# A two-layer hybrid attention backbone on one core: first loads ahead of the semaphore clearing, waits split by operand, and a changed order of work at the ends of phases

## The reference, cut to what matters

```python
for layer in range(DEPTH):
    need_ctx = layer < DEPTH - 1
    h_l = modulate(x, norm1_g[layer], sh1, sc1)        # rmsnorm(x, g) * (1 + scale) + shift
    h_c = modulate(xc, norm1_g[layer], csh1, csc1)
    ...                                                # o_l, o_c: the two attentions of the layer
    x = x + g1 * (o_l @ w_out[layer])
    x = x + g2 * sq_relu_mlp(modulate(x, norm2_g[layer], sh2, sc2), mlp_w1[layer], mlp_w2[layer])
    if need_ctx:
        xc = xc + cg1 * (o_c @ w_out[layer])
        xc = xc + cg2 * sq_relu_mlp(modulate(xc, norm2_g[layer], csh2, csc2), mlp_w1[layer], mlp_w2[layer])
return x

def diff_attend(q, k, v, lam):
    s = jnp.einsum('bqhtd,bkhtd->bthqk', q, k).astype(jnp.float32) * (q.shape[-1] ** -0.5)
    a = jax.nn.softmax(s, axis=-1)
    p = a[:, 0] - lam * a[:, 1]
    return jnp.einsum('bhqk,bkhe->bqhe', p.astype(v.dtype), v)
```

## Time and profile before

| | us |
|---|---|
| three runs before | 3991.56, 3997.02 (median), 3999.05 |
| profiled execution: its own time | 3994.86 |
| its span in the trace | 3993.1 |
| PE busy | 3593.2 (90%) |
| DVE busy | 2000.9 (50%) |
| ACT busy | 1297.3 (32%) |
| POOL busy | 172.7 (4%) |
| mean granted clock of PE | 0.945 |

### The profile page before, as it was taken

One profiled execution on the slowest core, in us unless ns is written; L12 is line 12 of the kernel. 1 busy time (PEld: TensorE's weight loads), 2 busy tenths in 40 slices (PEclk: granted clock), 3 DMA queues, 4 the chain that ended last, 5 costly groups with the idle time before them and its releaser, 6 DMA issues. The chain is left out here.

```text
span 3993.1 us, 47823 instructions
## 1 busy us (share of the span) xinstructions
PE 3593.2 (90%) x17926; PEld 2880.8 (72%) x17926; DVE 2000.9 (50%) x2900; ACT 1297.3 (32%) x2312; POOL 172.7 (4%) x186
## 2 busy tenths in 40 slices
PE   8779798696989999999988889699699889999999
PEld 2567666585778888888867778477466678888887
DVE  2564365586654444443455356488444363333333
ACT  2453244464431111111125445466333351111111
POOL 0200020000120000000001000000000020000000
PEclk9899899898999999999998989799799899999999
DMA  8344453442322222222214344333344331111112
GB/s 306 130 152 161 132 119 86 102 98 78 90 72 68 66 68 59 60 60 60 61 52 154 138 153 136 85 72 71 79 99 90 99 97 48 45 47 47 50 53 69
DMA packets 438709, 370.72 MB, mean 93 GB/s; under 512 B 103302, under 2 KB 382614, under 8 KB 433430
## 3 DMA queue, kind: packets, MB, share of 16 engines
q1 hardware_dynamic: 438549, 368.61, 32.7%
HBM read 280.86 MB, written 87.69 MB: 92 GB/s over the span
## 5 line engine op out<-in xcount | busy, mean ns | idle before, releaser
L2022 DVE SCALAR_TENSOR_TENSOR xT<-ps,mods,xT 128x1024 f32<-128x1024 f32 x192 | 189.3, 1014 | 420.8 <-PE ps L2236 420.8
L2236 PE MATMUL ps<-e_gh,e_w2h 128*128 128x512 f32 x1280 | 355.6, 375 | 5.9 <-DVE e_w2l L2474 3.6
L2236 PE MATMUL ps<-e_gl,e_w2h 128*128 128x512 f32 x1280 | 351.7, 372 | 0.0
L2236 PE MATMUL ps<-e_gh,e_w2l 128*128 128x512 f32 x1280 | 351.3, 372 | 0.0
L2522 DVE TENSOR_TENSOR e_plain<-e_plain 128x1280 f32<-128x1280 f32 (+1 forms) x64 | 86.9, 1358 | 503.7 <-ACT e_plain L2389 503.7
L2236 PE MATMUL ps<-e_hh,e_w1h 128*128 128x512 f32 (+1 forms) x1200 | 329.2, 372 | 7.2 <-DVE e_w1l L2474 7.2
L2236 PE MATMUL ps<-e_hl,e_w1h 128*128 128x512 f32 (+1 forms) x1200 | 328.6, 371 | 0.0
L2236 PE MATMUL ps<-e_hh,e_w1l 128*128 128x512 f32 (+1 forms) x1200 | 328.2, 371 | 0.0
L2389 ACT ACTIVATE e_plain<-ps 128x1280 f32<-128x1280 f32 (+1 forms) x64 | 72.7, 1135 | 777.8 <-PE ps L2236 765.2
L2236 PEld LDWEIGHTS ps<-e_gh,e_w2h 128*128 128x128 f32 x1280 | 224.1, 189 | 55.3 <-DVE e_gl L2526 8.0
L2236 PEld LDWEIGHTS ps<-e_gl,e_w2h 128*128 128x128 f32 x1280 | 225.4, 189 | 43.4
(11 more groups left out here) (347 smaller groups left out, 7493.5 us busy)
## 6 DMA issues: line engine op xcount, KB each, us to landing
e_raw<-in_mlp_w SPq DMA_DIRECT2D x64, 512.0 KB, 4.2
e_raw<-in_mlp_w SPq DMA_DIRECT2D x128, 256.0 KB, 2.9
aw<-in_ada_w SPq DMA_DIRECT2D x12, 2048.0 KB, 9.2
e_raw<-in_w_out SPq DMA_DIRECT2D x48, 512.0 KB, 4.0
rstd<-in_ada_w SPq DMA_DIRECT2D x64, 384.0 KB, 3.4
qkC<-pc_stage SPq DMA_DIRECT2D x72, 192.0 KB, 2.7
hT<-pa_hb SPq DMA_DIRECT2D x10, 1024.0 KB, 5.4
qkA<-pa_stage SPq DMA_DIRECT2D x20, 512.0 KB, 3.2
```

The lines of the kernel that those rows point to most:

```text
L2022: ins = k.nc.vector.scalar_tensor_tensor(out=x, in0=ps, scalar=k.mods[:, layer, gate, bass.ds(n, 1), w], in1=x, op0=ALU.mult, op1=ALU.add)
L2236: mm = pe.matmul(k.ps[:, SB * (e % 2) + b, 0:n], w[:, e % 2, f], m[:, f, c0:c0 + n], start=(f == 0 and x == 0), stop=(f == nf - 1 and x == 2))
```

## The change

1. **Clearing behind loads.** `clear_before` stands behind the first loads in every phase: six weight slices in `pa`, `pb`, `pd`; three tiles of weights, the gains and rope in `pc`; the first head's loads in `ab`, `ac`, `ad`, `aa`; four row tiles and two weight tiles in the two `e`.
2. **Waits by operand.** `load_head` raises a near semaphore (what the rough products read) and a far one (the rest and the values). In `aa`, q's first 512 columns and k of map 0, those of map 1, and the rest (v, q's other columns) have one each, with 13 loads per head in place of 11; in `ac` 5 in place of 3. The score of a head's first step, and the cast of the values, wait for far.
3. **Tables.** `ab`'s two masks are one load, with the sinks behind the first head; `ad`'s three are one; `aa`'s lambda constants come behind the first head.
4. **project's order.** The jobs of tiles 0 and 1 alternate: (0,0), (1,0), (0,1), (1,1), ... The second half of h(2) is built after job 3 (`pa`) or 5 (`pd`) (`split_at`). In `pd` the reciprocals of the norm (L696) are made per 128 tokens, ten in place of three, between the h of the tiles.
5. **layer_end's order.** Row tiles 0, 1 before weight tile 0, tiles 2, 3 before tile 1; roots and norm of a row tile one unit earlier; beside the units only part 0's h is built (u 10 to 13, and 16 to 19 in layer 1), part 1's after the loop; (1,0) before the sums, (0,2)'s weights cut ahead of the first relu; `next_sums` adds the last feature tile's squares by three more matmuls instead of a last accumulation on DVE.

```diff
-    jobs = [(t, j) for t in range(NT) for j in range(U) if t < LT or not units[j].latents]
+    jobs = [(t, j) for j in range(U) for t in range(2)] + [(t, j) for t in range(2, NT) for j in range(U) if t < LT or not units[j].latents]
+    split_at = [first_of[0]] + [max(first_of[t], last_of[t - 1] + 1) for t in range(1, NT)]
...
-                k.phases.clear_before(sp)
...
                     sp.dma_start(raw[:, x % RAW, 0:u.width], w_dram[f, :, col0 + u.c0:col0 + u.c0 + u.width]).then_inc(wr[x % RAW], 16)
+                    if x == RAW - 1:
+                        k.phases.clear_before(sp)
...
-                    if keeps_h and n == first_of[t] and t + 1 < NT:
-                        modulate(t + 1, range(KT // 2, KT))
+                    for x in range(NT - 1):
+                        if keeps_h and n == split_at[x]:
+                            modulate(x + 1, range(KT // 2, KT))
...
+                def inverse(t):
+                    if sums_at is not None and t < NT:
+                        q = slice(t * P, (t + 1) * P)
+                        dve.wait_ge(s.std, t * P // 512 + 1)
+                        nc.vector.reciprocal(k.rstd[:, q], k.rstd[:, q]).then_inc(s.rec, 1)
...
                     if u % NQ == 0:
-                        pe.wait_ge(s.ld0 if p == 0 else s.ld1, i * 16 * loads + 16 * loads)
+                        pe.wait_ge(s.ld0 if p == 0 else s.ld1, i * 16 * near + 16 * near)
...
+                    if x % NS == 0:
+                        pe.wait_ge(s.lf0 if p == 0 else s.lf1, i * 16 * far + 16 * far)
...
-        p, n = u // KT - 1, u % KT
-        return [(p, f) for f in (2 * n - 4, 2 * n - 3)] if p >= 0 and 2 <= n < 2 + KT // 2 else []
+        f = 2 * (u - (KT + 2 if SB == 3 else 2 * KT))
+        return [(0, f), (0, f + 1)] if 0 <= f < KT else []
...
                 fetch_rows(0)
+                fetch_rows(1)
...
                 fetch_out(0)
-                fetch_rows(1)
+                fetch_rows(2)
+                fetch_rows(3)
                 fetch_out(1)
-                for t in range(2, min(nt, RB + 4)):
+                k.phases.clear_before(sp)
+                for t in range(4, min(nt, RB + 4)):
...
-                    t = turned_beside(u)
+                    t = turned_beside(u + 1)
...
-                    pe.wait_ge(s.acc2, KT)
+                    pe.wait_ge(s.x, x_nth(C - 1, KT - 1))
+                    pe.wait_ge(s.acc2, KT - 1)
...
                         early(0, 0)
+                        early(1, 0)
                         sums(NP - 1)
-                        for p in range(1, NP - 1):
+                        for p in range(1, NP):
                             early(0, p)
-                        for p in range(NP - 1):
                             early(1, p)
-                        early(0, NP - 1)
-                        early(1, NP - 1)
```

More of the change, by code:

```diff
@@ L119, in shape_constants @@
     before, after = np.where(c >= q, 0, MASKED), np.where(c <= q, 0, MASKED)
-    out["wmask"] = np.stack([before, after], 1).astype(np.float32)
-    out["wband"] = np.stack([after.T, np.zeros((P, P)), before.T], 1).astype(np.float32)
+    out["wtab"] = np.stack([before, after, after.T, np.zeros((P, P)), before.T], 1).astype(np.float32)
     cq, ck = np.arange(GRID_W)[:, None], np.arange(GRID_W)[None, :]
@@ L125, in shape_constants @@
     col = np.where((ck >= cs) & (ck < cs + NA_COLS), 0, MASKED).astype(np.float32)
-    out["cmask"] = np.concatenate([col, col], 0)
-    out["cmaskT"] = np.tile(col.T, (2, 2))
     first, last = np.zeros((2, P, P), np.float32)
@@ L133, in shape_constants @@
     last[:, GRID_W:] = MASKED
-    out["rmask"] = np.ascontiguousarray(np.stack([first, last, first.T, last.T], 1))
+    out["ntab"] = np.concatenate([first, last, first.T, last.T, np.tile(col.T, (2, 2)), np.concatenate([col, col], 0)], 1).astype(np.float32)
     return out
@@ L720, in _ @@
                         before = None
-                    if keeps_h and n == first_of[t] and t + 1 < NT:
-                        split_h(t + 1)
+                    for x in range(NT - 1):
+                        if keeps_h and n == split_at[x]:
+                            split_h(x + 1)
+                            inverse(x + 2)
                 if before is not None:
@@ L1302, in attend @@
     EB, OB, TB = 5, 6, 7
-    loads = load_head(None, None, None, None, None, None)
+    near, far = load_head(None, None, None, None, None, None)
     last_step = [max(x for x in range(V) if (x // NS) * NB + head_steps[x % NS].block == b) for b in range(BLOCKS)]
@@ L1369, in attend @@
             b_sb, bT = sb("b", [P, 2, BR, GRID_W], F32R), sb("bT", [P, 2, 2, ND, P], F32R)
-            cmask, cmaskT = sb("cm", [P, GRID_W]), sb("cmT", [P, P])
             rmask = sb("rm", [P, 4, P], F32R)
-        mtab = sb("mtab", [P, 5, P]) if sink is not None or bias is not None else None
-        tables = 3 if sink is not None or bias is not None else 0
+        mtab = sb("mtab", [P, 6, P]) if sink is not None or bias is not None else None
+        tables = 2 if sink is not None else 1 if bias is not None else 0
+        if bias is not None:
+            cmaskT, cmask = mtab[:, 4], mtab[:, 5, 0:GRID_W]
         if beside is not None:
@@ L1448, in pair @@
                         fetch(0, 0, False)
+                        if sink is not None:
+                            sp.dma_start(sinks[:], sink.unsqueeze(0).broadcast_to([P, heads])).then_inc(s.tab, 16)
+                        k.phases.clear_before(sp)
                         fetch(0, 1, False)
@@ L1581, in values_high @@
                 def values_high(i, p):
-                    act.wait_ge(s.ld0 if p == 0 else s.ld1, i * 16 * loads + 16 * loads)
+                    act.wait_ge(s.lf0 if p == 0 else s.lf1, i * 16 * far + 16 * far)
                     nc.scalar.copy(vh[:, p], v_sb[:, p]).then_inc(s.vh, 1)
@@ L1743, in stacked_loader, with load @@
 def stacked_loader(qk, q_base, k_index, v_dram, v_index, v_width, n_q):
-    def load(sp, i, p, places, _, sem):
+    def load(sp, i, p, places, near, far):
         if sp is None:
-            return 6
+            return 3, 3
         q_sb, k_sb, v_sb, q_top, k_top = places
@@ L1897, in values @@
                     pe.wait_ge(s.ev, turn_nth(i, v, c))
+                    if c == 0 and v % NQ == 0:
+                        pe.wait_ge(s.lf0 if v < NQ else s.lf1, (i + 1) * 16 * 3)
                     if c == 0 and (i or v):
@@ L2250, in next_sums @@
                 def next_sums():
-                    pe.wait_ge(s.acc2, KT)
+                    pe.wait_ge(s.x, x_nth(C - 1, KT - 1))
+                    pe.wait_ge(s.acc2, KT - 1)
                     for b, (c0, n) in enumerate(chunks):
-                        mm = pe.matmul(k.ps[:, NEXT_BANK + b, 0:n], k.ones[:], sqx[:, 2, c0:c0 + n], start=True, stop=True)
+                        pe.matmul(k.ps[:, NEXT_BANK + b, 0:n], k.ones[:], sqx[:, 2, c0:c0 + n], start=True, stop=False)
+                    pe.wait_ge(s.sq2, KT)
+                    for b, (c0, n) in enumerate(chunks):
+                        mm = pe.matmul(k.ps[:, NEXT_BANK + b, 0:n], k.ones[:], sqx[:, (KT - 1) % 2, c0:c0 + n], start=False, stop=True)
                     mm.then_inc(s.sum2, 1)
@@ L2371, in _ @@
                         modulate(p, f)
+                cut(0, 1, True)
                 square(NU - 1)
+                for f in range(KT):
+                    modulate(NP - 2, f)
                 deviation(NP - 1)
-                cut(0, 1, True)
                 for f in range(KT):
@@ L2380, in chunk @@
                         if e + 1 < U:
-                            if not (first and e == 0):
-                                cut(c, e + 1, first)
+                            if not (first and e == 1):
+                                cut(c, e + 2 if first and e == 0 else e + 1, first)
                         elif not last:
@@ L2503, in _ @@
                 add_out(NU - 1)
+                cut(0, 1)
                 accumulate(NU - 2)
                 accumulate(NU - 1)
+                for f in range(KT):
+                    split(NP - 2, f)
                 inverse(NP - 1)
-                cut(0, 1)
                 for f in range(KT):
@@ L2513, in chunk @@
                         if e + 1 < U:
-                            if not (first and e == 0):
-                                cut(c, e + 1)
+                            if not (first and e == 1):
+                                cut(c, e + 2 if first and e == 0 else e + 1)
                         elif not last:
```

73 lines of the change are left out of this document (36 added, 37 removed).

## The result

| | median us | lowest to highest | ratio to before, 95% interval |
|---|---|---|---|
| before, runs beside this one | 3998.03 | 3991.56 to 3999.14 | |
| changed | 3955.06 | 3952.21 to 3958.08 | 0.9897 [0.9882, 0.9912] |

A forecast was written before the change was run, and what follows sets the result against it. PE bounds the kernel, busy 3593.2 of 3993.1 us; the change can move its idle time and slower running behind pauses. Terms sum to -37.8: 3957 against the profiled 3994.9, 3959 against the median; range 3935 to 3981.

The forecast's parts named there:

- pa: Projection pa: one more job behind the wait for h(1), slower matmuls, later h(2), less the clears: +8.8 us.
- pd: Projection pd: loss between +5 and +10 from the job order, with reciprocals made smaller ahead of h(0): +8 us.
- pc: Phase pc: gains only the clears moved behind the first loads, -2.2 us.
- aa: Phase aa: first maxima start once the lambda constants, last of 14 loads, land and their chain ends: -4.1 us.
- `ad` steady: Later heads in ad: the six waits on v all go except some tenths, -9 us.
- `ac`'s start: Start of ac: PE waits only for near loads, 2.6 from clears plus 5.4, -8.0 us.
- first `e`: First layer end: waits near unit 18 and ahead of the MLP's third unit go, with smaller terms: -10.4 us.
- Rival A: Lambda and sinks loads land early though issued last; aa gains 10 us, ab 7: 3942, chance 0.12.
- Rival B: In pa, pb and pd the order's delay comes with every tile, +60 in place of +17: 4002, chance 0.05.
- Rival C: The order of tiles costs nothing; pa and pd at -2 each: 3939, chance 0.12.
- Rival D: Starts of ad and ac give half, the two e a third: 3986, one alone 3973; chance 0.25 in part or whole.
- Rival E: Whole kernel: no change, the terms cancel within 8 us; chance 0.05.

The follow-up runs named there:

- clear_front: The changed kernel with the clearing of semaphores back at the front of every phase: 3967.33 us, ratio 0.992.
- rough_waits_far: The changed kernel whose rough products in ac and ad wait for all loads of the head again: 3976.62 us, ratio 0.9948.
- order_back: The changed kernel with the old order of jobs in the projections (tile by tile): 3933.46 us, ratio 0.9836.
- built_back: The changed kernel with part 1's h in layer_end built beside the units again, nothing of it behind the loop: 3968.16 us, ratio 0.9933.
- turn_late: The changed kernel with roots and norm of a row tile one unit later, as before: 3946.93 us, ratio 0.9876.
- three_edits: The kernel of order_back_small_first with roots and norm of a row tile one unit later too: 3909.44 us, ratio 0.9783.
- recip_back: The changed kernel with layer 1's reciprocals as before, three of 512 tokens ahead of all else on DVE in pd: 3953.09 us, ratio 0.9886.
- small_first: The changed kernel with the lambda load ahead of aa's first head and the sinks load ahead of ab's: 3939.13 us, ratio 0.9855.
- order_back_small_first: The changed kernel with the old job order in the projections and the lambda and sinks loads ahead of the first heads: 3919.03 us, ratio 0.9801.

## Why the prediction was right, and where it was not

The forecast of 3959 lies 4 us from 3955.06. In the profiled executions the sum was -37.8 and -40.6 came. Part of that closeness is luck. `ad` steady (6.5), `ab` (2.6) and the two `e` (2.7) gained more than forecast; `pc` (+5.0), `pa` (+2.5) and an opening that took 1.9 longer in this execution, for which the sum had no term, took it back. The account of where time would be won and lost held in the main. Step by step, forecast against the trace (and the run that isolates it):

- `ac`'s start: -8.0, came -8.3 (5.8 of it the split, 2.8 the clears; q and k had landed 5.8 us behind their first issue where I had 6.0). `ad`'s start: -10.0, came -9.1 (6.6 the split, 0.9 the clears). `aa`: -4.1, came -4.1, though its parts were off: counted from `ab`'s last product (694.54 before, 703.42 after, from the traces), the constants landed 27.4 us on where I had 30.0, and the first maxima came at 28.9 instead of 35.3, 6.4 earlier; 2.3 were lost again inside. The 2.2 that I took for the clears in `aa` no run shows: `clear_front` has the constants no later.
- `ad` steady: -9, came -15.5. All six waits went, 11.3 where I had taken 9; the term that was missing is PE's slower work, 4.3 us in this pair of traces, most of it in one fall of the clock. `rough_waits_far`, which brings six waits back, gives 9.5 of waits and 1.7 of slower work.
- `ab`: -1.5, came -4.1, of which 3.6 at the start, where clears are 2.4. `pb`: 0 came as -2.4 + 2.2.
- `pa`: +8.8, came +11.3. The clears didn't bring the first product forward, which waits for h's chain and the weights behind it, 9.22 us in both profiles; but the first job is shorter, 9.6 us instead of 11.3, so that something of their 1.6 seems to have come inside the phase (it took 10.7 in the second profile of before; PE's clock differs there between executions, and how much is due to it these runs can't say). The order cost 13.0 against `order_back` where I had 10.4. 12.6 of it are idle time, so my 1.9 for slower matmuls was not there: the rows that I took it from have 0.79 us already behind a pause of 5.79. What I had too small is h(2), for which PE now waits 6.06 instead of 1.28.
- `pd`: +8, came +7.7, as -1.6 at the start and +9.3 inside. The start is due to the reciprocals and not to the clears, and they take it back inside; the order is 9.6.
- `pc`: -2.2 as the start showed, but +4.9 inside, so +2.8. This is the step of the sum that failed in sign, and its cause stays open. PE's idle time inside is 29.3 and 30.6 us in the two profiles of before and 32.7 to 35.7 in those of all twelve other kernels; ACT waits there for its own stores (`qkC`) to land, 22.2 and 23.8 us before, 24.6 to 26.5 in the others. Undone alone, it isn't pc's own program (`clear_front` has before's and 230.6), the order (232.2), `layer_end` (230.6), the reciprocals (227.5) or the tables (231.0), and it isn't a single execution (225.4 in the second one of before).
- first `e`: -10.4, came -12.4: -15.7 up to the MLP's first product with `w2`, and +3.1 from there to the last such product, where nothing was changed. The wait of 6.36 ahead of the next sums did not shrink to nearly zero but to 4.85. Second: -9.4, came -10.1. `built_back` shows most of it to be what is built beside the units, as forecast.
- Rival A (small loads overtake): not where it counted. In `aa` 128 KB issued last landed last, and in `ab` the sinks, 4 KB, landed 0.2 us behind v. The order isn't strict, though: at `ad`'s start a bias load of 224 KB issued 0.6 us after v landed 1.3 us before it (2859.71 and 2861.01, kernel before). The Trainium skill, page "DMA: Bandwidth & Descriptors", section "Queues, rings and completion order", says that completion is "not FIFO per issuing engine". These landings agree with it.
- Rival B (a delay with every tile) is refuted: from (3,0) on PE's waits for h in `pa` are at most 1.3 us a tile, as before, and in `pd` there is one more, of 3.7, and then none. Rival C (the order costs nothing) is refuted: what it priced at 21 us is what `order_back` takes away. Rival D: no far wait took the place of a near one in `ac` or `ad`, and the two `e` gained what was forecast. Rival E: the whole moved by 43 us.

## What to carry to other kernels

When waits are split so that the first product waits for less, list what else the first step of every engine needs: a load of 128 KB moved to the end of the queue took back two thirds of the gain in `aa` (9.1 of 13.2 us), and one of 4 KB 3.0 us in `ab`. An order that alternates two tiles pays only if both tiles' operands are there; where the second is computed during the first, the second unit's work on tile 0 is what fills the wait. Six waits of 1 to 2 us on PE cost 1.7 us more than their own 9.5 in the run that isolates them, and 4.3 more than their 11.3 where the clock fell behind one; so look at the clock of the rows behind a wait before pricing it.

## What was not expected of the hardware

The MLP of the first `e`, from its first product with `w2` to its last, has the same instructions in all kernels, and no waits but 3.6 us in each, yet took from 875.2 us (`turn_late` and `three_edits`) over 881.5 (twice, in both profiles of before) and 884.5 (changed) to 886.0 (`recip_back`). Four of its eight chunks in windows for the changed kernel, and three for `turn_late` (columns as above):

```profile
1309.60:1425.80 116.20, 115.75 (x602) 98.20 (x601) 52.16 (x58) 13.58 (x16) 0.00 (x0) 1.00 0.22 64
1425.80:1542.10 116.30, 115.85 (x603) 98.30 (x602) 52.19 (x58) 13.58 (x16) 0.00 (x0) 1.00 0.22 63
1542.10:1659.80 117.70, 117.26 (x602) 99.34 (x601) 52.07 (x58) 13.58 (x16) 0.00 (x0) 0.99 0.22 62
1659.80:1779.20 119.40, 118.94 (x602) 100.84 (x601) 52.19 (x58) 13.58 (x16) 0.00 (x0) 0.97 0.22 61
```

```profile
1309.60:1425.80 116.20, 115.74 (x602) 98.21 (x601) 52.11 (x58) 13.58 (x16) 0.00 (x0) 1.00 0.23 64
1425.80:1542.10 116.30, 115.84 (x603) 98.33 (x602) 52.27 (x58) 13.57 (x16) 0.00 (x0) 1.00 0.22 63
1542.10:1658.30 116.20, 115.74 (x602) 98.22 (x601) 52.09 (x58) 13.57 (x16) 0.00 (x0) 1.00 0.22 63
```

A chunk takes 116.2 us at a granted clock of 1.00 and 1.5 or 3 more where that falls to 0.99 or 0.97, with PE busy all the time. The last of the four, cut finer:

```profile
1659.80:1705.80 46.00, 45.55 (x243) 38.80 (x242) 24.48 (x31) 5.74 (x8) 0.00 (x0) 1.00 0.30 85
1705.80:1712.60 6.80, 6.80 (x21) 5.70 (x22) 0.59 (x1) 0.00 (x0) 0.00 (x0) 0.51 0.43 135
1712.60:1779.20 66.60, 66.60 (x341) 56.34 (x340) 27.11 (x27) 7.85 (x8) 0.00 (x0) 1.00 0.14 37
```

So the 0.97 is one stretch of some 7 us at 1.2 GHz, the lower of the clock's two levels, between 46 and 67 us at the full one; PE had not paused since the 0.5 us at the chunk's beginning. The traces have one such stretch in the MLP of `turn_late` and of `three_edits`, three in those of `order_back` and `small_first` (878.3 us), four in before's, six in the changed kernel's and eight in `recip_back`'s. Most last some 3 us and cost 1.5. Their number and length account for the differences in the MLP's time.

Both kernels with the later norm were some 8 to 10 us faster in the median, of which the output product explains 0.6 to 5.0 (the stretch before the first product with `w2` takes 204.8 us in `three_edits` and 209.8 in `order_back_small_first`). Why a shift of a few small instructions ahead of the MLP should go with fewer falls within it, these runs do not tell. It also means that single differences under some 8 us between kernels of this length are no evidence for an edit unless the phase itself shows them.
